# Modulation matrices in a two-block network: ScalarE scales the slices in place, GpSimd adds them, TensorE sums partitions for three chunks at a time

## The reference, cut to what matters

```python
def adaln(c, w, b):                 # w: (1024, 3072), four of them
    m = jax.nn.silu(c.astype(jnp.float32)) @ w + b
    shift, scale, gate = jnp.split(m, 3, axis=-1)
```

## Time and profile before

| what | value |
|---|---|
| three runs | 1980.46, 1980.88, 1988.24 us |
| median | 1980.88 us |
| profiled execution: span from the first to the last instruction | 1980.0 us |
| TensorE busy in the span | 1919.8 us, 97% |
| VectorE, ScalarE, GpSimd busy | 35%, 19%, 6% |
| first layer, second layer of the first block | about 10 to 311 us, 315 to 611 us |
| mean granted TensorE clock | 0.984 of full speed |

### The profile page before, as it was taken

How to read it: one execution, slowest core, us unless ns; L and a number is a source line. 1 busy time by engine, 2 the same in 40 slices (tenths; PEclk the granted TensorE clock), 3 DMA queues, 4 the chain that set the end, 5 groups by cost and what they waited for, 6 DMA issues and landing times.

```text
span 1980.0 us, 28488 instructions
## 1 busy us (share of the span) xinstructions
PE 1919.8 (97%) x11940; PEld 1070.5 (54%) x11940; DVE 689.7 (35%) x1472; ACT 372.2 (19%) x776; POOL 115.0 (6%) x98
## 2 busy tenths in 40 slices
PE   7999999999998999999989988999999999999998
PEld 6577866577865765776756544232323233333332
DVE  3364414354413573434449943010101010101112
ACT  3322102222103232234320012010101010101011
POOL 0000010000010000000016620000000000000000
PEclk9999999999999999999999998999999999999999
DMA  9255574264673316533323135999989999999993
GB/s 359 94 218 208 222 296 170 95 245 182 243 290 128 128 43 246 191 159 128 127 106 126 45 149 202 365 378 376 374 374 375 374 369 382 366 379 364 389 368 143
DMA packets 44037, 483.98 MB, mean 244 GB/s; under 512 B 5108, under 2 KB 6772, under 8 KB 10328
## 3 DMA queue, kind: packets, MB, share of 16 engines
q1 hardware_dynamic: 39136, 471.73, 59.2%
q10 hardware_dynamic: 4248, 9.07, 1.3%
q0 software_dynamic: 576, 2.10, 0.3%
HBM read 479.07 MB, written 10.10 MB: 247 GB/s over the span
## 4 chain that ended last, share of the span: by engine, by line
PE 88%; DVE 6%; DMA 3%; issue 1%; ACT 1%; ACTq 1%; POOL 0%; DVEq 0%; SPq 0%
PE bank L921 20%; PE bank L579 14%; PE bank L951 12%; PE bank L874 8%; PE bank L886 4%; PE bank L738 3%; PE bank L571 3%; PE bank L564 3%; PE bank L744 3%; PE bank L592 2%; PE bank L1000 2%; DMA arena<-bias_rows 1%; PE bank L1095 1%; PE bank L560 1%; PE bank L1028 1%; PE bank L935 1%
## 5 line engine op out<-in xcount | busy, mean ns | idle before, releaser
L921 PE MATMUL bank<-arena 128*32 128x512 f32 x4096 | 457.3, 592 | 0.0
L579 PE MATMUL bank<-arena 128*128 128x256 f32 x1408 | 313.3, 382 | 0.0
L921 PEld LDWEIGHTS bank<-arena 128*32 128x32 f32 x4096 | 136.1, 110 | 300.3 <-issue 300.3
L579 PEld LDWEIGHTS bank<-arena 128*128 128x128 f32 x1408 | 265.5, 190 | 54.2 <-issue 15.8
L951 PE MATMUL bank<-arena 128*32 128x512 f32 x2112 | 238.2, 595 | 0.0
L2077 DVE TENSOR_TENSOR arena<-arena,bank 128x256 f32<-128x256 f32 x64 | 27.0, 421 | 562.1 <-ACT arena L1447 511.6
L874 PE MATMUL bank<-arena 128*128 128x256 f32 x704 | 153.7, 379 | 0.1
L874 PEld LDWEIGHTS bank<-arena 128*128 128x128 f32 x704 | 133.6, 190 | 21.8 <-issue 4.1
L951 PEld LDWEIGHTS bank<-arena 128*32 128x32 f32 x2112 | 62.9, 109 | 133.3 <-issue 132.7
L1447 ACT ACTIVATE arena<-bank 128x256 f32<-128x256 f32 x64 | 24.6, 385 | 517.5 <-PE bank L921 517.4
L2323 POOL TENSOR_TENSOR arena<-arena 128x512 f32<-128x512 f32 x64 | 81.3, 1270 | 293.4 <-DVE arena L2131 290.9
(11 more groups left out here) (446 smaller groups left out, 1894.4 us busy)
## 6 DMA issues: line engine op xcount, KB each, us to landing
arena<-in_wgu SPq DMA_DIRECT2D x88, 2048.0 KB, 10.2
arena<-in_w SPq DMA_DIRECT2D x46, 2048.0 KB, 8.1
arena<-in_wdn SPq DMA_DIRECT2D x88, 1024.0 KB, 9.6
arena<-in_modw SPq DMA_DIRECT2D x24, 2048.0 KB, 9.3
arena<-in_wf SPq DMA_DIRECT2D x11, 3072.0 KB, 10.4
arena<-in_flt_deltas ACTq DMA_DIRECT2D x2, 1024.0 KB, 11.7
slot_rows<-arena ACTq DMA_DIRECT2D x7, 192.0 KB, 3.5
cst<-in_consts SPq DMA_DIRECT2D x1, 1162.0 KB, 7.7
```

Of the source, the lines that this page charges most:

```text
L579: ins = mm(bank[b][:, j * S:(j + 1) * S], w[:, col:col + P], hT[:, k, :], start=(k == 0), stop=(k == KT - 1))
L921: ins = mm(bank[w % 2][32 * j:32 * j + 32, :], hTe[:, k, TOK * b:TOK * b + TOK], wslot[SLOT[c]][:, k, :], start=(k == 0), stop=(k == KT - ...
```

## The change

The modulation chunks are taken off TensorE but for a last sum.

- ScalarE: at step ("proj", m + 4, 0) for m = 0 to 8, and at (PA, 1), (PA, 3), (PH, 3) for m = 9 to 11, it multiplies the eight slices of chunk m in place by silu(c), eight instructions on 128x512, each waiting for the one before. This stands before what ScalarE does for the group of that step.
- GpSimd: adds the two halves of the chunk (128x2048), then halves of that (128x1024), then 128x512 into `mod_sums[m]`, each waiting for the one before.
- TensorE: four "modmul" steps in a layer instead of twelve, before groups 13, 22, 26 and 34. Each waits for the sums of three more chunks and issues four matmuls of 32 output rows, with a constant column of ones.
- VectorE: adds the bank of each of the four to `modsum` (L1598 ff. of the new kernel); ScalarE's twelve copies and GpSimd's twelve adds of before are gone.
- SyncE's queue: the load that follows a modulation chunk in its buffer waits for GpSimd's sum instead of TensorE's group.
- The constants grow by 64 columns, `band` and its memset go, and the sums lie in parts of the arena that are free at that time, with a wait each.

```diff
+MOD_SETS = 4
+MOD_OF = MOD_CHUNKS // MOD_SETS
+MOD_AT = {13: 0, 22: 1, 26: 2, 34: 3}
+GROUPS_1 = 36 + MOD_SETS
...
+MOD_SCALE = {("proj", m + 4, 0): m for m in range(9)}
+MOD_SCALE.update({("proj", PA, 1): 9, ("proj", PA, 3): 10, ("proj", PH, 3): 11})
...
-        c, h = step[1:]
-        if c >= 4 and h == 0:
-            m = c - 4
-            out.append(("modmul", m, 0))
+        if n in MOD_AT:
+            out.append(("modmul", MOD_AT[n], 0))
...
-                    sp.wait_ge(sm["grp_ps"], l * GROUPS_1 + LOAD_END[n - RING])
+                    if LOADS[n - RING][0] == "w":
+                        sp.wait_ge(sm["grp_ps"], l * GROUPS_1 + LOAD_END[n - RING])
+                    else:
+                        sp.wait_ge(sm["mod_sum"], l * MOD_CHUNKS + LOAD_END[n - RING])
...
-                        pe.wait_ge(landed[at % RING], l * (16 * LOADS_1 // RING) + 16 * (at // RING + 1))
-                        for k in range(KT):
-                            r = slice(32 * (k % 4), 32 * (k % 4) + 32)
-                            ins = mm(bank[n % 2][r, :], band[:, k, 31 - c:63 - c], ring[at % RING][:, k * 512:(k + 1) * 512],
-                                     start=(k < 4), stop=(k >= 4), skip_group_check=True)
+                        pe.wait_ge(sm["mod_sum"], l * MOD_CHUNKS + MOD_OF * (c + 1))
+                        for q in range(4):
+                            m = MOD_OF * c + min(q, MOD_OF - 1)
+                            col = C_BAND + (31 - m if q < MOD_OF else 32)
+                            ins = mm(bank[n % 2][32 * q:32 * q + 32, :], cst[:, col:col + 32], mod_sums[m],
+                                     start=True, stop=True, skip_group_check=True)
...
-                        pe.wait_ge(sm["mod_in"], (l + 1) * MOD_CHUNKS)
+                        n = GROUP[("modmul", MOD_SETS - 1, 0)]
+                        pe.wait_ge(free[n % 2], l * (GROUPS_1 // 2) + n // 2 + 1)
...
+            def modulation(l, m):
+
+                at = PLACE[("m", m)]
+                act.wait_ge(landed[at % RING], l * (16 * LOADS_1 // RING) + 16 * (at // RING + 1))
+                w = ring[at % RING].rearrange("p (k n) -> p k n", k=KT)
+                for k in range(KT):
+                    ins = F(w[:, k, :], w[:, k, :], ACT.Copy, scale=silu_c[:, k:k + 1])
+                    if k < KT - 1:
+                        link(ins)
+                ins.then_inc(sm["mod_scaled"], 1)
...
+                    if step in MOD_SCALE:
+                        modulation(l, MOD_SCALE[step])
...
-                    elif name == "modmul":
-                        n = GROUP[step]
-                        act.wait_ge(sm["grp_ps"], l * GROUPS_1 + n + 1)
-                        if l * MOD_CHUNKS + c >= 2:
-                            act.wait_ge(sm["mod_in"], l * MOD_CHUNKS + c - 1)
-                        F(modout[:, c % 2, :], bank[n % 2][:, :], ACT.Copy).then_inc(free[n % 2], 1)
...
+                    elif name == "modmul":
+                        n = GROUP[step]
+                        dve.wait_ge(sm["grp_ps"], l * GROUPS_1 + n + 1)
+                        if c == 0:
+                            if l:
+                                dve.wait_ge(sm["mod_ps"], l)
+                            ins = v.tensor_copy(modsum, bank[n % 2][:, :])
+                        else:
+                            ins = v.tensor_tensor(modsum, modsum, bank[n % 2][:, :], ALU.add)
+                        ins.then_inc(free[n % 2], 1)
+                        out_of(l, step)
...
+            for l in range(DEPTH):
+                for m in range(MOD_CHUNKS):
+                    pool.wait_ge(sm["mod_scaled"], l * MOD_CHUNKS + m + 1)
+                    if m == 0 and l:
+                        pool.wait_ge(sm["grp_ps"], l * GROUPS_1)
+                    elif m in (2, 3):
+                        pool.wait_ge(sm["fp_ps"], l * 8 + 8)
+                    elif m in (4, 5, 8, 9):
+                        pool.wait_ge(sm["grp_ps"], l * GROUPS_1 + GROUP[("modmul", (m - 4) // MOD_OF, 0)] + 1)
+                    elif m in (6, 7):
+                        pool.wait_ge(sm["wg_ready"], l * 4 + 4)
+                    elif m >= 10:
+                        pool.wait_ge(sm["yt_ps"], l * 2 + 2)
+                    w = ring[PLACE[("m", m)] % RING]
+                    for half in (2048, 1024):
+                        link(pool.tensor_tensor(w[:, 0:half], w[:, 0:half], w[:, half:2 * half], ALU.add))
+                    pool.tensor_tensor(mod_sums[m], w[:, 0:512], w[:, 512:1024], ALU.add).then_inc(sm["mod_sum"], 1)
+                    pool.wait_ge(sm["mod_sum"], l * MOD_CHUNKS + m + 1)
```

More of the change, by code:

```diff
@@ L48 @@
     0, 128, 256, 384, 896, 1408, 1920, 2432, 2688, 2690, 2708, 3220, 3284)
-C_UP, C_LM, C_S4 = 3285, 3413, 3605
-C_N = 3637
+C_UP, C_LM, C_S4, C_BAND = 3285, 3413, 3605, 3637
+C_N = 3701
 HV, Q, K_, V, HX1, HX2, ZA, ZH, GA0, GA1, GH0, GH1, PA, PH, WO0, WO1 = range(16)
@@ L111 @@
 YSQ = {GROUP[("proj", WO0 + i, t)]: 2 * t + i + 1 for t in range(TT) for i in range(2)}
-LOAD_END = [max(n for (name, c, _), n in GROUP.items() if name == {"w": "proj", "m": "modmul"}[kind] and c == chunk) + 1
+LOAD_END = [max(n for (name, c, _), n in GROUP.items() if name == "proj" and c == chunk) + 1 if kind == "w" else chunk + 1
             for kind, chunk in LOADS]
@@ L261, in model @@
         modsum = view(att + 4096, 512)
-        band = view(att + 4608, KT, 63)
-        modout = view(att + 5120, 2, 512)
+        early_sums = [view(at, 512) for at in (att + 4608, att + 5120)]
+        mod_sums = early_sums + [view(at, 512) for at in (big1 + 3072, big1 + 3584)] + early_sums\
+            + [view(at, 512) for at in (att, att + 512)] + early_sums + [view(at, 512) for at in (att + 2048, att + 2560)]
+        silu_c = ev[:, E_C:E_C + KT]
         biasr = view(LOW + 3072, 4, TT, S)
@@ L357, in model @@
                 on_ready yt_ps ya_ready
-                macc_used mod_ps mod_in mask_landed gb_in gb_ps gb_ready
+                macc_used mod_ps mod_sum mask_landed gb_in gb_ps gb_ready
                 gla_ps gla_act gla_in gla_done cl_ready fsc_ps fsc_ready fpr_ready fw_ready ft_ps fpt_ready fva_ps
-                fo_out lev_in lev_exp lev_ready lev_ps lev_used go_ps gn_ready gt_ps mix_ready
+                fo_out mod_scaled lev_in lev_exp lev_ready lev_ps lev_used go_ps gn_ready gt_ps mix_ready
                 h_ps sil_ready hid_ready dn_ps b5_landed c5_landed s5_step s5_act c5_ready b5_ready b5_ps
                 b5t_ready sv_used sv_ps cz_ready y_out sy_ps gelu_ready glu_ready tb_arg tb_ready iota_ready
-                w_ready z5_ready rt_ps rt_step rt_act items_ready oh_ready ga_ps hte_ready pt_ps pt_ready ysb_ready back_ps low_ready rows_out row_of rows_in stored c_ready
+                z5_ready rt_ps rt_step rt_act items_ready oh_ready ga_ps hte_ready pt_ps pt_ready ysb_ready back_ps low_ready rows_out row_of rows_in stored c_ready
                 x_part nstd_ready hta_ready ystd_ready ysq_ready dn_half
@@ L1225, in _ @@
                             act.wait_ge(sm["z_ready"], l * 4 + 4)
+                            act.wait_ge(sm["grp_ps"], l * GROUPS_1 + GROUP[("modmul", 2, 0)] + 1)
                             if l + 1 < DEPTH:
@@ L1256, in _ @@
                                 act.wait_ge(sm["ev_landed"], 16)
-                                F(band[:, :, 31:32], ev[:, E_C:E_C + 8].unsqueeze(2), ACT.Silu).then_inc(sm["c_ready"], 1)
+                                F(silu_c, silu_c, ACT.Silu).then_inc(sm["c_ready"], 1)
+                                act.wait_ge(sm["c_ready"], 1)
                         elif c in (ZA, ZH):
@@ L1560, in _ @@
             link(v.memset(small[:, :], 0.0))
-            link(v.memset(band.rearrange("p a b -> p (a b)"), 0.0))
             v.memset(small[:, 95:96], 1e-6).then_inc(sm["x_ready"], 1)
@@ L2301, in _ @@
             link = Chain(pool, sm["pool_chain"])
-            for n in range(DEPTH * MOD_CHUNKS):
-                g = GROUP[("modmul", n % MOD_CHUNKS, 0)]
-                pool.wait_ge(free[g % 2], n // MOD_CHUNKS * (GROUPS_1 // 2) + g // 2 + 1)
-                if n % MOD_CHUNKS == 0:
-                    if n:
-                        pool.wait_ge(sm["mod_ps"], n // MOD_CHUNKS)
-                    ins = pool.tensor_copy(modsum, modout[:, n % 2, :])
-                else:
-                    ins = pool.tensor_tensor(modsum, modsum, modout[:, n % 2, :], ALU.add)
-                ins.then_inc(sm["mod_in"], 1)
-                pool.wait_ge(sm["mod_in"], n + 1)
+            for l in range(DEPTH):
[16 more added lines that the diff above has]
+                    pool.wait_ge(sm["mod_sum"], l * MOD_CHUNKS + m + 1)
             pool.wait_ge(sm["xt_ps"], 16)
@@ L2396 @@
              _np.triu(_np.ones((P, P)), 1), _np.broadcast_to(_np.concatenate([late3, late3, _np.arange(SLOTS), late3]), (P, 2 * SLOTS)),
-             _np.tile(_np.eye(TOK), (P // TOK, 1))]
```

(1 more changed line is left out.)

4 lines of the change are left out of this document (removed).

## The result

The changed kernel takes 2049.52 us (median of four, 2048.02 to 2054.63) against 1982.62 us for the kernel before beside it: a ratio of 1.033, 95% interval 1.031 to 1.035. Forecast were 2037 us in a range of 1995 to 2058.

A forecast was written before the change was run, and what follows sets the result against it. TensorE was taken to bound the stage. A layer: -18.5 us freed, +36.9 waits, +9.6 clock, so +28.0; two layers +56, giving 2037 us, in a range of 1995 to 2058.

The forecast's parts named there:

- freed on TensorE: Modmul steps: 22.2 us a layer before, 3.7 after, so 18.5 us a layer won if all the rest is hidden.
- (a): First mix: VectorE stands still beside GpSimd's adds, so TensorE's weigh after HX1 waits 5.9 us.
- (b): Modmul 0 before group 13: TensorE waits 14.3 us for m2's sum, 2.1 of it from VectorE's dft instructions.
- (c): Idft before group 20: VectorE's chain is held up by m5's adds, so TensorE waits 6.3 us.
- (d): Modmul 2 before group 26, on m6 to m8: TensorE waits 8.35 us for m8's sum.
- (e): Read-out of PH behind an add 0.6, WO0 0.75, group 34 0.7: together 2.05 us.
- clock: After long idle stretches TensorE runs at a lower clock: 2.4 us for each of four waits, 9.6 us a layer.
- Rival 1: GpSimd and VectorE don't delay each other for long: +8.3 us a layer, 1997.5 us; chance 0.12.
- 2: As Rival 1, with ScalarE and GpSimd at their lower bounds (4.9 and 7.1): +3 us a layer, 1987; chance 0.07.
- Rival 3: Faster: scaling and adding at 3 us a chunk for both engines, m2's sum early for modmul 0: 1947 us; chance 0.05.
- Rival 4: VectorE keeps its turn and GpSimd starves through the dft chain: some 2040, up to 2060; no chance of its own.
- Rival 5: Slices are scaled late since they land late; dismissed, as m2 is asked for 25 us before scaling; no chance given.

The follow-up runs named there:

- e6: Changed kernel with GpSimd's 2048- and 1024-column additions left out: 2159.50 us.
- e2: Changed kernel with GpSimd's wide adds cut into pieces of 128x512, sets in their places: 2028.38 us, ratio 1.023.
- e3: Changed kernel with sets before groups 16, 24, 29, 34, and GpSimd waiting for VectorE's mixes and dft chains before m0, m1, m2, m5: 1980.77 us, ratio 0.999.
- e10: Changed kernel with set 0 alone moved, from group 13 to group 16: 2031.89 us.
- e9: Changed kernel with set 1 alone moved, from group 22 to group 24: 2042.09 us.
- e1: Changed kernel with its four sets before groups 16, 24, 29 and 34 instead of 13, 22, 26 and 34: 2008.98 us, ratio 1.013.
- e11: e7 with weight chunks issued ahead of modulation chunks from chunk 5 on, chunks 5 and 6 scaled one projection group later: 1988.46 us, ratio 1.002.
- e4: Changed kernel with sets before groups 14, 24, 29, 34, GpSimd waiting for VectorE before chunks 0, 1, 5, and chunk 2 scaled a step earlier: 1972.32 us, ratio 0.994.
- e7: e4 with the additions of chunks 9, 10 and 11 alone in 512-column pieces: 1970.15 us, ratio 0.993.
- e5: Changed kernel with wide additions in 512-column pieces and sets at groups 16, 24, 29 and 34: 1988.28 us, ratio 1.003.
- e8: Kernel before the change with four of the eight matmuls of each modulation set left out: 1972.36 us, ratio 0.994.

## Why the prediction came out as it did

The forecast held: slower, by the mechanism named, 12.5 us from the centre, on the low side. By layer 2, point by point:

| Term, us | predicted | measured | shown by |
|---|---|---|---|
| freed on TensorE | -18.5 | -17.9 | e6, busy time |
| (a) weigh after HX1 | 5.9 | 4.96 | L704, 0.65 in e2, gone in e3 |
| weigh after HX2 | none | 2.36 | L704, gone in e2 and e3 |
| (b) set 0 | 14.3 | 11.10 | L600, gone in e10 |
| (c) second inverse DFT | 6.3 | 5.77 | L683, gone in e3 |
| bank of set 1 | none | 5.87 | L589, gone in e9 |
| (d) set 2 | 8.35 | 8.19 | L600, gone in e1 |
| (e) PH, WO0, group 34 | 2.05 | 1.50 | L574, less the 0.92 of before |
| clock | 9.6 | 11.0 (layer 1: 13.6) | busy time |
| **layer** | **+28.0** | **+32.2** (layer 1: +40.4) | L526 against L516 |

The column of what was measured adds up to 32.2 with the 18.5 from which the clock's 11.0 is reckoned; with e6's 17.9 the clock would have 10.4.

That the layer came within 4.2 us is in part luck. The five waits that were forecast are 5.4 us shorter in sum than forecast; the two that were not forecast bring 8.2, and the clock 1.4 more.

*The scaling and the adds.* A chunk's scaling took 5.99 us (6.0 predicted), its adds 8.3 unhindered (8.63). The smallest L2346, the add of 1024 columns, took 2.34 us, which leaves about 4.5 of 6.95 for the widest. The Trainium skill (GPSIMD Engine Reference, Performance versus the Vector engine) gives 4.497 us for it, and the trace agrees with that better than with the prediction's 4.8. What the prediction makes of this figure is a little small: 0.4 us a chunk, at (a) to (d) in two layers, is 3 us, not 2.

*The turns.* They are as predicted: one VectorE instruction between two adds. The Trainium skill (SBUF — State Buffer, Who interferes with whom) has a lock that is held for a whole instruction; the rows agree, with 4.48 us against 0.35 beside a wide add and 1.24 beside a narrow one.

*Term (b) was too large*, in two of its parts. GpSimd's three adds took 8.9 us in place of 10.7, for the 2.1 us put down to VectorE's instructions were 0.6. And TensorE arrived 1.8 us later, since the groups behind earlier waits ran in part at the lower clock (8.73 us for the one at 477.68, where 7.17 are usual). The waits are not independent: one that delays TensorE shortens the next.

*The step that failed* is "VectorE's four additions (0.69 each) stand in for twelve ScalarE copies; both lie beside groups of 7 us". The duration was right and the place was not read: VectorE takes set 1's bank out only behind the heads' turn and the second chain, which is itself stretched by 5.7 us beside chunk 7's adds. It cost 5.87 us and 7.6 with the clock (e9), more than (a). Counting instructions that cost nothing is not enough where the engine is changed: the new engine's order decides when the bank comes free. The second omission, 2.36 us at the weigh after HX2, is (a)'s mechanism a second time, which I had let hit once.

*The clock.* The price of a wait was about right and the number of waits was not: busy time shows 11.0 and 13.6 us where 4 x 2.4 were taken; there are six such waits in layer 2, so some 2 us for each (2.3 and 1.7 by the two stretches shown at e9). The granted clock over 90 to 640 us was 0.92, not 0.97 (0.99 before). The new TensorE matmuls took 12.0 us in sum, not 7.4: two of the four sets of a layer stand right behind a wait and take 1.94 us each, the other two 1.06.

*The rivals.* Rival 1 and with it 2 fall by e2 and e3: take the collisions away and 21 or 28 us go. Rival 3 falls by the measured 5.99 and 8.3 us, where it needed 3 for each engine. Rival 4, in which GpSimd starves through a VectorE chain, does not show: beside the forward DFT the two wide adds took 7.26 in place of 6.95. Rival 5, late loads, has no part in TensorE's waits in the changed kernel's layer 2, but it decided e11. What was said of SyncE's loads, "3 to 4 us of cover at the narrowest", holds for the changed kernel, where no group behind a modulation chunk waits for weights; it is used up as soon as TensorE stops waiting elsewhere (e3, e4, e7).

Layer 1 lost 8.2 us more than layer 2, 5.6 of it idle time and 2.6 busy time. Its timeline shows where:

```profile
49.52 5.40 PE L617 MATMUL bank<-arena,cst 128*128 128x512 f32 x8 [3.85 <-DMA arena<-bias_rows]
...
141.76 0.66 PE L704 MATMUL bank<-cst,arena 128*128 128x128 f32 x4 [3.34 <-DVE arena L1757]
...
311.94 7.17 PE L581 MATMUL bank<-arena 128*128 128x256 f32 x32 [2.07 <-DVE arena L1648]
```

The first wait is 2.2 us longer than before (1.67), and its matmuls take 1.6 more (3.80 before). But in the executions of e1, e9 and e10 this wait is 1.55, 0.68 and 0.64, so it goes with the execution and not with the change. The second is 1.0 longer than in layer 2. The third, a group of PH that waits for a read-out beside an addition, is missing in layer 2; it belongs to term (e). The last 0.4 us of idle time are at the first loads. Open is why the same read-outs meet the additions a little otherwise in the two layers, and where 1.0 us of the busy time comes from.

## What to carry to other kernels

Work that is moved from the bounding engine to idle ones is paid for at the places where it meets them: list for each moved instruction who waits behind it on its new engine, for banks as much as for data, and where a wide operation of GpSimd meets VectorE's SBUF operations. The same arithmetic cost 3.3% here in one order and gained 0.6% in another (e4, e7). When a freed microsecond doesn't appear, compare busy and idle time of the bounding engine by stage: it tells clock, waits and real work apart, where the total mixes them.

## What the runs showed of the hardware beyond what was expected

- Cutting an add of 2048 and one of 1024 columns into six of 512 costs GpSimd 1.0 us (8.00 against 6.97 when nobody is beside). The longest that a VectorE instruction of 0.69 us took beside an add fell from 4.60 us (L1648 in layer 1) to 1.76 (L1698); L1755, 0.35 alone, fell from 4.48 to 1.24.
- The clock's loss went more with the number of TensorE's waits over 2 us in layer 2 than with their length: three of 29 us together lost 6.5 us of busy time (e2), five of 28 lost 9.2 (e10), five of 22.6 lost 10.9 (e1), each reckoned as 18.5 less the fall in busy time. These are single executions.
- The run time of this kernel depends on its values: e6 did a quarter more expert matmuls.
- Some executions lose about 4.7 us in the second block whatever is done in the first: a wait for weights of 2.4 to 2.8 us in place of 0.2 to 0.6 and slower matmuls behind it (e5, e8, e9, e11). A difference of that size between two medians says little until the stage has been looked at.
